# One weight sum of each feed-forward item moved from VectorE to GpSimd

## The reference

```
h = modulate(rms_norm(x, g_ffn1), sh1, sc1)
x = x + 0.5 * (1 + ga1) * swiglu(h, w1_gate, w1_up, w1_down)
def swiglu(h, w_gate, w_up, w_down):
    return (jax.nn.silu(h @ w_gate) * (h @ w_up)) @ w_down
```

## Time and profile before

| | us |
|---|---|
| median of 3 runs | 2441.39 (2439.96 to 2443.12) |
| profiled execution | 2439.12 |
| its span, first to last instruction | 2437.3 |
| TensorE busy | 2158.9 (89%) |
| VectorE busy | 974.4 (40%) |
| ScalarE busy | 509.0 (21%) |
| GpSimd busy | 0.2 |
| mean granted TensorE clock | 0.957 of 2.4 GHz |

### The profile page before, as it was taken

How to read it: one execution, slowest core, us unless ns; L and a number is a source line. 1 busy time by engine, 2 the same in 40 slices (tenths; PEclk the granted TensorE clock), 3 DMA queues, 4 the chain that set the end, 5 groups by cost and what they waited for, 6 DMA issues and landing times.

```text
span 2437.3 us, 34407 instructions
## 1 busy us (share of the span) xinstructions
PE 2158.9 (89%) x14427; PEld 1511.1 (62%) x14427; DVE 974.4 (40%) x1725; ACT 509.0 (21%) x1052; POOL 0.2 (0%) x4
## 2 busy tenths in 40 slices
PE   7999999999999999999999998777777777777776
PEld 4888888666564888888754554444444444444443
DVE  4777753145443543453223525322232222222223
ACT  3111100244323111110221422211111111111112
POOL 0000000000000000000000000000000000000000
PEclk9999999999999999999999999988998989998998
DMA  7565721411202224212401044999999999999997
GB/s 280 187 228 174 250 95 48 104 37 42 96 1 69 69 70 151 70 66 78 148 14 69 1 190 181 427 427 428 429 427 430 428 429 429 427 430 428 429 429 298
DMA packets 150550, 549.06 MB, mean 225 GB/s; under 512 B 9376, under 2 KB 102832, under 8 KB 124736
## 3 DMA queue, kind: packets, MB, share of 16 engines
q1 hardware_dynamic: 150464, 547.83, 57.1%
HBM read 545.71 MB, written 2.10 MB: 225 GB/s over the span
## 4 chain that ended last, share of the span: by engine, by line
PE 62%; DMA 30%; DVE 4%; ACT 1%; issue 1%; SPq 1%; ACTq 0%; PEldq 0%; DVEq 0%; PEld 0%
DMA slots<-in_expert_w_up 27%; PE ps L854 18%; PE ps L897 11%; PE ps L1410 8%; PE ps L944 4%; PE ps L1342 2%; PE ps L1035 2%; PE ps L1120 2%; PE ps L950 2%; DMA slots<-in_w_mod 2%; PE ps L968 1%; PE ps L1115 1%; PE ps L1118 1%; PE ps L977 1%; DMA slots<-in_expert_w_down 1%
## 5 line engine op out<-in xcount | busy, mean ns | idle before, releaser
L1410 PE MATMUL ps<-slots,xT 128*32 128x256 f32 x4032 | 292.8, 454 | 188.9 <-DMA slots<-in_expert_w_up 169.4
L1410 PEld LDWEIGHTS ps<-slots,xT 128*32 128x32 f32 x4032 | 158.3, 130 | 311.3 <-issue 176.8
L854 PE MATMUL ps<-hT,slots 128*128 128x256 f32 x1408 | 314.1, 381 | 6.5 <-ACT hT L1543 3.6
L854 PEld LDWEIGHTS ps<-hT,slots 128*128 128x128 f32 x1408 | 267.8, 191 | 46.5 <-ACT tmp L1564 4.5
L854 PE MATMUL ps<-slots 128*128 128x256 f32 x1056 | 238.0, 382 | 5.6 <-DVE slots L1972 5.6
L854 PEld LDWEIGHTS ps<-slots 128*128 128x128 f32 x1056 | 201.7, 192 | 33.8 <-issue 6.3
L2514 DVE COPY hT<-ps 128x128 f32<-128x128 f32 x64 | 18.5, 289 | 418.1 <-PE ps L1417 418.1
L2520 DVE TENSOR_TENSOR big<-ps,big 128x512 f32<-128x512 f32 x128 | 88.3, 691 | 219.0 <-PE ps L1445 219.0
L1831 ACT ACTIVATE xT<-ps 32x256 f32<-32x256 f32 x256 | 96.2, 376 | 259.5 <-PE ps L1430 257.3
L1430 PE MATMUL ps<-slots,hT 128*32 128x256 f32 x2040 | 123.3, 381 | 30.0 <-DVE hT L2514 29.5
L1825 ACT ACTIVATE big<-ps 32x256 f32<-32x256 f32 x128 | 48.0, 375 | 392.4 <-PE ps L1410 391.6
(11 more groups left out here) (381 smaller groups left out, 2562.1 us busy)
## 6 DMA issues: line engine op xcount, KB each, us to landing
slots<-in_expert_w_gate SPq DMA_DIRECT2D x63, 2048.0 KB, 18.4
slots<-in_expert_w_up SPq DMA_DIRECT2D x63, 2048.0 KB, 22.8
slots<-in_expert_w_down SPq DMA_DIRECT2D x63, 2048.0 KB, 24.7
slots<-in_w_mod SPq DMA_DIRECT2D x18, 2048.0 KB, 11.5
slots<-in_w_gate SPq DMA_DIRECT2D x22, 1024.0 KB, 5.5
slots<-in_w_up SPq DMA_DIRECT2D x22, 1024.0 KB, 8.1
slots<-in_w_down SPq DMA_DIRECT2D x8, 2816.0 KB, 10.2
slots<-in_w_in SPq DMA_DIRECT2D x24, 512.0 KB, 5.6
```

Of the source, the lines that this page charges most:

```text
L854: last = mm(bank[:, g], lhs[:, g, k], rhs[:, k], start=(first and g == 0 and k == 0), stop=(k == 3), skip_group_check=True)
L1410: last = mm(ps[at:at + CAP, j, 0:256], xsT[:, k, i * CAP:(i + 1) * CAP], w[g][k][:, 256 * h:256 * (h + 1)], start=(k == 0), stop=(k == KC ...
```

## The change

Sum 2 of every gate-up item and of every down item is issued by GpSimd. It keeps its place and its operands, waits for sum 0 of its item (the only other reader of low1), and signals a semaphore of its own. s_ws now counts three sums per item; TensorE's M7 waits for the new semaphore in place of s_ws, and M3 for the third value of s_ws.

```
+        s_wd = sem("weight_difference_ready")
-        SUMS = 4 * (N_ITEM + N_DOWN)
+        SUMS = 3 * (N_ITEM + N_DOWN)
+        DIFFS = N_ITEM + N_DOWN
 # TensorE, gate_up and down
-                pe.wait_ge(s_ws, sums + 3)
+                pe.wait_ge(s_wd, diffs + 1)
...
-                pe.wait_ge(s_ws, sums + 4)
+                pe.wait_ge(s_ws, sums + 3)
 # VectorE, gate_up_sum (down_weight_sum likewise, L2000)
-                elif i == 2:
-                    v.tensor_tensor(low[..., P:2 * P], low[..., 0:P], low[..., P:2 * P], ALU.subtract).then_inc(s_ws, 1)
 # VectorE, ffn
-                gate_up_sum(r, 0, 2)
...
-                        for i in range(3):
+                        for i in range(2):
                             gate_up_sum(r, n + 1, i)
 # GpSimd
-            for n in (2, 8, 10):
-                phase_end(pool, n)
+            def ffn(r):
+                for n in range(N_ITEM):
+                    low = gu_view(n % 2)[:, :, 0:4, :]
+                    pool.wait_ge(s_ws, SUMS * r + 3 * n + 1)
+                    nc.gpsimd.tensor_tensor(low[..., P:2 * P], low[..., 0:P], low[..., P:2 * P], ALU.subtract).then_inc(s_wd, 1)
+                for d in range(N_DOWN):
+                    w = down_view(d)
+                    pool.wait_ge(s_ws, SUMS * r + 3 * (N_ITEM + d) + 1)
+                    nc.gpsimd.tensor_tensor(w[:, 0::2, P:2 * P], w[:, 0::2, 0:P], w[:, 0::2, P:2 * P], ALU.subtract).then_inc(s_wd, 1)
+            phase_end(pool, 2)
+            ffn(0)
+            phase_end(pool, 8)
+            ffn(1)
+            phase_end(pool, 10)
```

More of the change, by code:

```diff
@@ L856, in product @@
                     last.then_inc(s_pr, 1)
-                sums, copies = SUMS * r + 4 * n, 4 * (N_ITEM * r + n)
+                sums, diffs, copies = SUMS * r + 3 * n, DIFFS * r + n, 4 * (N_ITEM * r + n)
                 pe.wait_ge(s_gw[n % 2], gu_filled(r, n))
@@ L898, in product @@
                     last.then_inc(s_pr, 1)
-                sums, added, hidden, tokens = SUMS * r + 4 * (N_ITEM + d), N_PROD * (N_DOWN * r + d), 4 * N_ITEM * r, TOKEN_SUMS * r + 4
+                sums, diffs = SUMS * r + 3 * (N_ITEM + d), DIFFS * r + N_ITEM + d
+                added, hidden, tokens = N_PROD * (N_DOWN * r + d), 4 * N_ITEM * r, TOKEN_SUMS * r + 4
                 pe.wait_ge(s_dw[d % 2], down_filled(r, d))
@@ L1943, in gate_up_sum @@
                 w = gu_view(n % 2)
-                done = SUMS * r + 4 * n
+                done = SUMS * r + 3 * n
                 low, high = w[:, :, 0:4, :], w[:, :, 4:8, :]
@@ L1988, in down_weight_sum @@
                 w = down_view(d)
-                done = SUMS * r + 4 * (N_ITEM + d)
+                done = SUMS * r + 3 * (N_ITEM + d)
                 if i == 0:
@@ L1998, in down_weight_sum @@
                     v.tensor_tensor(down_sum[1], down_sum[0], w[:, 0::2, 0:P], ALU.subtract).then_inc(s_ws, 1)
-                elif i == 2:
-                    v.tensor_tensor(w[:, 0::2, P:2 * P], w[:, 0::2, 0:P], w[:, 0::2, P:2 * P], ALU.subtract).then_inc(s_ws, 1)
                 else:
```

## The result

The changed kernel takes 2453.98 us (median) against 2441.72 us of the kernel before, timed together: ratio 1.0048, 95% interval 1.0033 to 1.0063, so 8 to 15 us slower. One of its five executions, 3167.9 us at a granted clock of 0.65, is left out of the ratio; the other four took 2450.89 to 2457.59 us. The forecast was 2454.6 us.

What follows compares the result with a forecast made beforehand. TensorE was taken to bound the kernel, with a few waits for VectorE's work; pairs 6.0, heads 4.5 and clock 2.7 us summed to 13.2 us slower, 2454.6 us on the median's scale, range 2436 to 2461 us.

Steps and rivals of the forecast that it cites:

- What bounds the kernel: Feed-forwards: TensorE bounds the second; in the first, four waits for VectorE's modulation work really cost 3.94 us.
- the six places named: Four pairs of modulation items in the first feed-forward and the heads of both feed-forwards, where time would be lost.
- GpSimd's D: Duration of one gate-up sum 2 on GpSimd: between 1.22 and 2.26 us, upper end taken.
- The stall: Behind sum 1, VectorE stands still for the whole GpSimd sum, 2.26 us; full stall given 0.45.
- Heads: Start of each feed-forward: token sum L1972, and TensorE with it, comes 2.26 us later; 4.5 us in both.
- Clock: First feed-forward's head: a 4.3 us TensorE wait lowers its clock, slowing the 32 matmuls behind by 2.75 us.
- Pairs: Before modulation items 2, 4, 6, 8 of the first feed-forward: later start and later load, 4 x 1.50 = 6.0 us.
- the load's lost lead: Modulation load's 1.16 us lead on the weights' loads shrinks by 0.75 us, so it lands another 0.38 us later.
- Rival 1: Both engines read SBUF side by side, VectorE is not held: 3.8 us less, 2437.6 us; chance 0.32.
- Rival 2: GpSimd gives way to VectorE's back-to-back instructions; M7 of the first item may wait up to 1 us: 2438.5 us; chance 0.08.
- Rival 3: GpSimd starts over 3.4 us after release, sparing the first head: 8.3 us slower, 2449.7 us; chance 0.10.

Runs made afterwards that it cites:

- first item back: Changed kernel with sum 2 of item 0 of each feed-forward made by VectorE again: 2445.88 us, ratio 1.0020 to the kernel before.

## Why the prediction was right, and where its sizes were off

The time came out within 1 us of the forecast, and the mechanism is the one forecast, a stall of VectorE. But the terms did not all have their size, and part of the agreement is luck: as measured they make 9.4 us where 13.2 were forecast, and 2.3 us of the profiled executions that belong to no term fill much of the gap.

- What bounds the kernel: right. Only the six places named lose time; the second feed-forward's period and the down items (132.97 us before and after) are untouched, and M7 never waits for GpSimd. In a down step L2033 does not even move by the 1.6 us that I gave it: it reads PSUM and is not held.
- GpSimd's D, 2.26 us by the slowest VectorE row: 2.36 us alone, and 2.10 to 2.16 us as VectorE feels it. The estimate from the Trainium skill (GPSIMD Engine Reference, "Performance versus the Vector engine"), 2.25 us, agrees as well.
- The stall, which no row of before could decide: full. What the Trainium skill says of it (SBUF — State Buffer, "Who interferes with whom") is what the runs show, in the conditions that were tried: two SBUF inputs held (L1984, 1.98 us for 0.42), one SBUF input beside one in PSUM not (L2072, 0.69), GpSimd's reading holds (0.84 to 2.16 us), its writing beside a two-input sum doesn't.
- The reason for it, that the instructions around it all read two SBUF tensors, has a gap: in front of the pairs the held one is L1917 of the kernel before (L1920 in the changed one), which reads one. By that reason alone only the instruction behind it, which reads two and starts 0.51 us later in the kernel before (135.78 against 135.27 us), would have been held. That would have cost, as an estimate from these two starts, some 0.5 us less for each pair, 2 us in all. That the pairs' stall was full is luck in so far.
- Heads: 4.5 us forecast, 2.16 + 2.14 = 4.3 measured. Right, and undone by giving the first item back.
- Clock: 2.75 us forecast, 1.69 measured (8.83 - 7.14). The fall came, but the length of the wait, from which I took it, does not decide by itself: the clock fell behind 2.05 us in one kernel and not behind 2.06 in another, and behind 2.70, 2.73 and 2.83 us in a kernel where it did not fall behind 3.01. The price was taken from a head where the clock was low for longer (still 0.51 from 800 to 803 us); in the other kernels whose clock falls at the first head it is 1.5 to 2.4 us.
- Pairs: 6.0 us forecast, 3.46 measured (206.06 - 202.60). Each wait is 1.5 to 1.7 us, not 2 to 2.5. The stall is 0.16 us shorter than forecast, but the term most mis-sized is the load's lost lead, 0.38 us each. The lead shrank as forecast, from 1.16 to 0.41 us, but the loads did not take longer for it: the three loads that the two chains show take 7.77, 8.13 and 8.33 us before and 7.95, 7.83 and 7.94 after. So 4 x (2.10 - 1.14) = 3.8 us already covers the 3.46, and no run shows the 0.38.
- Sum: 4.3 + 1.7 + 3.5 = 9.4 us, against 11.8 between the two profiled executions. The rest lies where the programs don't differ: 1.25 us ahead of the first sum 0 (45.87 against 44.62 us), 0.9 us between the first feed-forward's items and the second head, and 0.2 us elsewhere. I take it for the scatter of single executions, which is not shown; 9.4 lies inside the interval of 8 to 15 us.

Rival 1 needed a stall under 0.76 us; it was 2.1. Rival 2 would have shown GpSimd's sum behind the token sums; it goes in ahead of the first of them, between two VectorE instructions that stand ready. Rival 3 needed a late start; it starts 0.15 us after its release. The gain that rival 1 counts is there, though, as soon as the hold is moved off the path: 2.8 of the 3.8 us.

## What to carry to other kernels

Moving a VectorE instruction to an idle GpSimd does not take it off VectorE's time line: while GpSimd reads SBUF, VectorE's instructions with two SBUF inputs (and here one with a single input) stand still, here 2.1 us for an instruction that had cost VectorE 1.14. What decides is what VectorE does next: start the GpSimd work, by one more wait, where VectorE idles or reads PSUM, and not at the event that also releases VectorE's own critical work. In a trace, look for the one VectorE instruction that is longer than its twins and ends soon behind a GpSimd record, and don't take GpSimd's recorded length for its work: it contains its own wait (3.31 to 3.40 us recorded here for 2.2 to 2.4 us of work).

## What the runs showed of the hardware that was not expected

- A GpSimd instruction that stands behind a running VectorE one goes in ahead of VectorE's next, even though that one was ready: sum 1 at 1.22 us, then GpSimd, then the held instruction. No waiting for a gap was seen.
- The one-input L1917 is held too (0.48 to 2.58 us). It has one SBUF tensor in and one out. It is also fast for its size, 484 ns for 512 elements where L1920 of the kernel before takes 752 and L2050 0.69 us, which may mean that it uses both paths. That was not tried.
- TensorE's clock can fall behind a wait of 2.05 us and stay up behind one of 3.01 us; what decides between these lengths was not found. At the first head one fall costs 1.5 to 2.4 us in the 32 matmuls behind it (8.64 to 9.57 us in place of 7.14).
